# Seven cache copies moved from SyncE's queue to ScalarE's, one or two ahead of each tile turn

## The reference, cut to what matters

```python
q, k, v, glu = _in_proj(x, w_in)                    # one projection, 2560 columns
att  = dilated_attention(q, k, v)                   # 8 heads x 64, three dilations
conv = silu(LN(depthwise_conv31(glu) + b))          # 512 channels
x1   = LN(ALPHA * x + concat(att, conv) @ w_out)
# PEER: 8 heads, product keys, the best 16 experts of 16384 per head and token
e, gate = route(x1)                                 # 128 experts per token
act  = gelu(sum_d x1[t, d] * expert_u[e[t, k], d])
y    = LN(ALPHA * x1 + sum_k gate * act * expert_v[e[t, k]])
# and, for the 8 sequences, the windows moved on by 8 positions:
new_k_sample = concat(cache_k_win, k_sample)[:, -2048:]
new_v_sample = concat(cache_v_win, v_sample)[:, -2048:]
```

## Time and profile before

| | |
|---|---|
| median of three runs | 3459.23 us |
| lowest, highest | 3455.15, 3467.26 us |
| the profiled execution, its own time | 3465.34 us |
| its span in the profile | 3463.5 us |
| DVE busy | 2709.9 us (78%) |
| PE busy | 2575.3 us (74%) |
| POOL busy | 1259.1 us (36%) |
| ACT busy | 718.4 us (21%) |
| moved by DMA | 1386.73 MB, mean 400 GB/s |

### The profile page before, as it was taken

The page is one execution under the profiler, slowest core; times in us unless marked ns, Lnnn a source line. Parts: engine busy times, 40 slices in busy tenths (PEclk is TensorE's granted clock), DMA queues, the critical chain, the costliest instruction groups (busy, mean ns, idle before and its releaser), DMA issues.

```text
span 3463.5 us, 39997 instructions
## 1 busy us (share of the span) xinstructions
PE 2575.3 (74%) x14040; PEld 1166.4 (34%) x14040; DVE 2709.9 (78%) x7309; ACT 718.4 (21%) x1565; POOL 1259.1 (36%) x1092
## 2 busy tenths in 40 slices
PE   6975588777767776777668767876787666789876
PEld 5544245322332333233324332433243322233321
DVE  5388788799799869996979699969996984345855
ACT  2210132023102310241005201520152002122100
POOL 0122123134434443444335444543444332224342
PEclk7998789888988897898788888998898888899999
DMA  9999899989999999999989999999999999999997
GB/s 334 383 409 416 347 390 367 424 318 421 421 412 365 421 421 421 395 416 421 420 343 399 421 421 398 417 421 421 392 416 421 421 408 422 419 419 398 417 390 329
DMA packets 218457, 1386.73 MB, mean 400 GB/s; under 512 B 28424, under 2 KB 39176, under 8 KB 67336
## 3 DMA queue, kind: packets, MB, share of 16 engines
q0 software_dynamic: 156672, 1140.92, 80.4%
q1 hardware_dynamic: 41040, 141.81, 10.7%
q10 hardware_dynamic: 20544, 101.45, 7.2%
HBM read 1370.99 MB, written 80.04 MB: 419 GB/s over the span
## 4 chain that ended last, share of the span: by engine, by line
DVE 38%; DMA 28%; PE 21%; issue 9%; ACT 2%; POOL 1%; SPq 0%; POOLq 0%; ACTq 0%; another core or an unknown queue 0%; DVEq 0%
DMA t<-in_expert_uv,t 26%; DVE t L1099 12%; PE psum L1477 10%; DVE t L966 4%; PE psum L1379 3%; PE psum L1420 3%; DVE psum L1126 2%; DMA t<-glu_scratch 2%; DVE t L1111 2%; DVE t L1047 2%; DVE t L1045 1%; DVE t L1048 1%; DVE t L1046 1%; DVE t L990 1%; PE psum L1301 1%
## 5 line engine op out<-in xcount | busy, mean ns | idle before, releaser
L645 POOL DMA_INDIRECT t<-in_expert_uv,t x1088 | 1258.9, 1157 | 2170.4 <-PE psum L1473 825.4
L1477 PE MATMUL psum<-t,t 64*64 64x512 f32 x4896 | 1356.6, 693 | 646.1 <-DVE t L1111 640.6
L1099 DVE CUSTOM_DVE_ANT_0 t<-t,t 128x1024 f32<-128x1024 f32 x1088 | 1322.9, 1222 | 462.5 <-DMA t<-in_expert_uv,t 441.7
L1477 PEld LDWEIGHTS psum<-t,t 64*64 64x64 f32 x4896 | 344.9, 149 | 1470.6 <-DVE t L1111 863.0
L1473 PE MATMUL psum<-t,t 64*64 64x512 f32 x2496 | 763.5, 741 | 0.0
L805 ACT ACTIVATE t<-t 128x2 f32<-128x2 f32 x544 | 110.8, 204 | 1851.5 <-DVE t L1099 1817.4
L1420 PEld LDWEIGHTS psum<-t,t 128*128 128x128 f32 x2304 | 274.1, 198 | 74.9 <-issue 66.8
L1301 PE MATMUL psum<-t,t 128*128 128x128 f32 (+2 forms) x768 | 257.1, 495 | 48.2 <-DMA t<-in_xT 41.7
L1420 PE MATMUL psum<-t,t 128*128 128x128 f32 (+1 forms) x2304 | 285.4, 284 | 2.6 <-ACT t L767 2.6
L966 DVE SCALAR_TENSOR_TENSOR t<-t,t,t 128x128 f32<-128x128 f32 x840 | 238.3, 346 | 0.0
L1301 PEld LDWEIGHTS psum<-t,t 128*128 128x128 f32 x768 | 132.0, 202 | 161.7 <-issue 118.5
(11 more groups left out here) (142 smaller groups left out, 2070.4 us busy)
## 6 DMA issues: line engine op xcount, KB each, us to landing
t<-in_wq_t ACTq DMA_DIRECT2D x65, 1024.0 KB
out<-in_cache_k_win SPq DMA_DIRECT2D x8, 4080.0 KB
out<-in_cache_v_win SPq DMA_DIRECT2D x8, 4080.0 KB
t<-in_w_in_t ACTq DMA_DIRECT2D x44, 512.0 KB, 11.4
t<-in_kc_t SPq DMA_DIRECT2D x8, 2560.0 KB
t<-in_vc_t SPq DMA_DIRECT2D x8, 2560.0 KB, 14.1
t<-in_expert_uv,t POOLq DMA_INDIRECT x1088
t<-in_w_v_t ACTq DMA_DIRECT2D x6, 1024.0 KB
```

Of the source, the lines that this page charges most:

```text
L645: pool.indirect_dma_start(ring[:, r, :], None, I["expert_uv"], bass.IndirectOffsetOnAxis(ap=idn[t % 2][:, s:s + 1], axis=0)).then_inc(land ...
L1099: dve.tensor_tensor_reduce(out=ring[:, r, 0:D], in0=x1[t % 2][:, :], in1=ring[:, r, 0:D], scale=1.0, scalar=0.0, op0=ALU.mult, op1=ALU.add ...
L1477: last = pe.matmul(MAIN[t][half][NS * a:NS * a + NS, :], zt[NS * a:NS * a + NS, k % Z_RING, j, :], vv[NS * a:NS * a + NS, :], start=(c == ...
```

## The change

Of the 16 cache copies SyncE keeps nine: five at the start instead of eight, three behind routed heads 1, 3 and 5 of tile 0 instead of four, and one in step 0, behind head 4 of tile 1's softmax, instead of four. The other seven are asked for by ScalarE, without any wait, at position 106 of its loop: two in step 0 and one in each of the steps 1 to 5. The copies themselves, their shape and the semaphore that they raise are the same.

```diff
+COPY_AT = 106
+TURN_COPIES = {0: (9, 10)} | {_n: (10 + _n,) for _n in range(1, 6)}
...
-            for i in range(PH):
+            for i in range(5):
                 if i:
                     sp.wait_ge(sm_done, i)
...
-            def cache_copies():
-                for i in (2, 5):
-                    sp.wait_ge(sm_done, PH + i)
-                    copy_cache(PH + 3 + (i + 1) // 3)
-                for i in (1, 4):
-                    sp.wait_ge(a_q, PH + i)
-                    copy_cache(PH + 6 + (i + 1) // 3)
...
-            for i in range(4):
-                sp.wait_ge(a_route, 2 * i if i else 1)
-                copy_cache(PH + i)
+            for i in range(3):
+                sp.wait_ge(a_route, 2 * i + 1)
+                copy_cache(5 + i)
...
                 if m == 1:
-                    cache_copies()
+                    sp.wait_ge(sm_done, PH + 4)
+                    copy_cache(8)
...
+            def copy_cache(i):
+                new, old = ((kc_o, I["cache_k_win"]), (vc_o, I["cache_v_win"]))[i % 2]
+                act.dma_start(new[i // 2].rearrange("t c -> (t c)").rearrange("(b a m) -> a b m", b=2, a=512),
+                              old[0, i // 2, NT:WIN].rearrange("t h e -> (t h e)").rearrange("(b a m) -> a b m", b=2, a=512)).then_inc(cache_out, 16)
...
+                        if 4 * g + i == COPY_AT:
+                            for k in TURN_COPIES.get(n, ()):
+                                copy_cache(k)
```

## The result

The kernel after takes 3510.3 us, median of six runs (3482.9 to 3524.6). The kernel before takes 3458.7 us in runs on the same chip (six, 3451.9 to 3467.3). The ratio is 1.0141, 95% interval 1.0109 to 1.0172: slower by 1.1 to 1.7%. I had forecast slower, 3478 us with a range of 3436 to 3506. The direction held and the size did not: 51.6 us lost where 19.4 were forecast, and the result lies above my range.

A forecast was written before the change was run, and what follows sets the result against it. Gathers hold the DMA engines for 80.4% of the span, so spare DMA time decides: -11 - 7 + 9 + 4 + 24.4 = +19.4 us on 3459.23 gives 3478.6, forecast as 3478 us, range 3436 to 3506.

The forecast's parts named there:

- First and second term: Steps -1 and 0: fewer early copies save 11 and 7 us, a third of 32.8 and 22.5 us possible.
- all that a lighter DMA load can give there is in these waits: Up to 735 us: gains can come only from VectorE's waits for gathers, together 55.3 us.
- Third term: Position 106 of step 0: the second copy's issue blocks ScalarE for 16.15 us, the gelu is late: +9 us.
- Fourth term: Turn of step 0: two copies need 19.8 us, find 15.8 us of hole, push the rest into step 1: +4 us.
- Fifth term: Steps 1 to 5, one copy each: 49.6 us of DMA time against holes of 25.2 us, so +24.4 us.
- VectorE does not starve at once: Position 106, steps 1 to 5: the copy draws on the nearly full ring, paid in the next DMA-bound part.
- Rival C: Turns: small load alternates with gather pieces, first tap waits; 21 to 42 us on top, 3500 to 3520 us; chance 0.17.
- The rule on packets: Small load at turns: whole packets would need four to seven turns and no tap waits; forecast preferred single pieces, 64 turns.

The follow-up runs named there:

- the four: Kernel with nine SyncE copies and four ScalarE copies in a row at position 106 of step 0, three windows not written: 3469.5 us, one run.
- eleven copies: The kernel after without the five single copies of steps 1 to 5, five output windows not written: 3435.1 us, ratio 0.9947 to the kernel before.
- the kernel with nine copies: The kernel after without ScalarE's seven copies, seven output windows not written: 3433.9 us, ratio 0.9934 to the kernel before.
- the tap comes late: The kernel after with the first convolution tap at position 6 of a step instead of 0: 3462.3 us, ratio 1.0013 to the kernel before.

## Why the prediction was wrong in size

**First and second term, -18: right.** The turn of step 0 came 18.2 us earlier. Without ScalarE's copies the whole kernel gained 22.5 us. The third that I took was a guess, though, and the place was only partly right: "all that a lighter DMA load can give there is in these waits" left out the first tap of step 0, whose wait fell by 7.3 us beside the 13 us of VectorE's waits for gathers.

**Third term, +9: failed.** "The second finds the queue occupied" held, and "the issue needs 16.15" did not. I carried over a row of SyncE's queue that had two copies ahead of it and not one. The second issue took 0.88 us, and only a third one blocked, with 16.29 us. Here the rule of the Trainium skill that I had put aside for those rows fits the pair and not the four: its page "DMA: Bandwidth & Descriptors", section "Issuing engines are not separate DMA queues", calls the cost of issuing usually small.

**Fourth term, +4: near enough.** Third and fourth together measured 1.2 us (4.5 by the ratios), not 13. The hole was larger than the 15.8 us that I had read, 29.6 us once the seven copies are gone, and the pair filled 19.2 of it.

**Fifth term, +24.4: the term that was mis-sized.** Its rule, that a copy fills the hole ahead of the turn and what finds no hole is paid in full, is what the pair shows, and step 1 in part: they cost 1.2 and 0.8 us. But for steps 2 to 5 I had counted holes that are no room. Of the 11.8 us of step 3, 10.5 are the idle stretch behind the late tap, with a share of 0.13 for 12 us. That is the price of a stop and not room for a copy, and my own rival C says so. The sum also set 11.8 us of hole against a copy of 9.9. In the 53 us ahead of these turns the share is 0.99 to 1.01 with eleven copies and 1.01 or 1.02 after. "VectorE does not starve at once" is contradicted too, by 8.8 us of waiting right behind the copy, and I found no debt that comes due later: from 1500 to 1640 us VectorE waits 27.7 us after and 27.4 before. The differences between steps of the profile after and those with eleven copies give the price, since each step has another mix:

- step 1, copy and no stop: +0.8 us
- step 4, copy and no stop: +9.1 us
- steps 2, 3 and 5, copy and stop: +19.8, +18.4, +18.9 us
- step 6, stop and no copy: +11.5 us

Four copies at 9 us and one at 1 are 37 us, not 24.4. With the 10.5 us taken out of the holes, my own sum would have been 49.6 - 14.7 = 34.9. Step 1 is the one in which VectorE has the most to do (318.0 us busy in the kernel with nine copies, where the later steps have 298 to 301).

**Rival C took place, with a chance of 0.17.** Its mechanism, its place and its price (21 to 42 us) are what was measured: four stops of 15 us, some 10 us each, and 38 us of them back in the steps behind them when the tap comes late. That its time (3500 to 3520) fits as well is in part luck: it stands on my sum, in which third and fourth term were 12 us too much and the fifth 13 us too little. The failure is in the weighing. The row with 15.35 us of waiting stood in the earlier trace rows, and the deciding point was written down: a backlog at the turn that outlasts 8.7 us. My own forecast left a backlog of 7 to 8 us by supposing that holes absorb the rest, and so the wrong fifth term held rival C down. With next to nothing absorbed, the backlog is nearly the whole copy, 9.9 us, and the rival is the likeliest case. The sum so mended is -22.5 + 1.2 + 37 + 4 x 10 = +56 against the measured 51.6; its last two terms come from single profiled executions.

**The rule on packets.** I had set single pieces taking turns against the skill's whole packets of 9 to 17 descriptors (same page, section "Queues, rings and completion order"). For the end of a late load the trace bears out the single pieces: gaps of 0.33 us, a gather's piece and a small one, and no groups of 9 to 17. For the whole load it bears out neither as I had put it. Some 980 of the 1024 pieces start between 3.8 and 11 us after the request, faster than one for one. Only the DMA engine that ends last takes its 64 turns, 64 x 0.33 = 21 us, and the load is as late as that one. Without a copy in the step the last piece starts after 9.8 to 11.9 us (in the kernel with nine copies).

**What stays open.** Why VectorE, which waited 0.3 us in this part of the step before, waits as soon as a copy starts; no run changed the ring's depth. Why one DMA engine ends so much later than the others, and why it doesn't at the turn of step 3 (3.97 us). And what the late tap would give with eleven copies, which no run tried.

## What to carry to other kernels

Before you count a gap in the DMA share as room, ask what made it. A gap ahead of the point where all engines meet did take copies here, two of them for about 1 us. A gap behind a late load was the price of waiting for it and took none, and where the share was full ahead of the turn a copy cost its whole transfer time. What such a copy delays most is not the bulk stream but the last pieces of a small transfer that someone waits for at once, so ask first which engine stops for it, and give that load fewer pieces or a later consumer. When a row already shows the rare long wait, price the forecast as if the change made it the usual one.

## What the runs showed of the hardware

- ScalarE's queue took two transfers of 1024 pieces in 0.70 and 0.88 us; the third and fourth blocked the engine for 16.29 and 13.63 us. The gelu behind them came after 31.26 us of idle time, where it is 7.80 us with two.
- A load of 64 small pieces for each DMA engine took 23.7 us beside full gathers, one of 40 pieces with the same bytes 13.9 us. At the stops over 980 of 1024 pieces had started by 11 us, and the last 40 or so came mostly 0.33 us apart, until 24 us.
- The state's load of 480 KB fell from 123.1 to 57.0 us when three copies fewer were asked for ahead of it.
- Two small loads asked for 16 us behind one of 1792 KB that took 39.8 us to land had issues of 9.19 and 9.30 us. Behind the same load, landing in 20.2 us, they had 0.56 and 0.62.
